# Chunked delta rule: half of the heads keep the matrices of the inverse on alternating halves of the partitions, and sums are made by identity products

## The reference, cut to what matters

```python
def step(state, inp):
    r_t, k_t, v_t, w_t, a_t, b_t = inp
    sa = jnp.einsum('bhvk,bhk->bhv', state, a_t)
    state = state * w_t[:, :, None, :] + sa[..., None] * b_t[:, :, None, :] + v_t[..., None] * k_t[:, :, None, :]
    return state, jnp.einsum('bhvk,bhk->bhv', state, r_t)
```

## Time and profile before

| | us |
|---|---|
| median of three runs | 1024.71 (1024.5 to 1026.01) |
| the profiled execution | 1027.42 |
| its span, from the first to the last instruction | 1025.6 |
| in it: PE busy | 901.2 (88%) |
| DVE busy | 448.3 (44%) |
| ACT busy | 333.9 (33%) |
| the inverse, from P2 to the start of WT | 488.27 to 525.81 |

### The profile page before, as it was taken

The page is one execution under the profiler, slowest core; times in us unless marked ns, Lnnn a source line. Parts: engine busy times, 40 slices in busy tenths (PEclk is TensorE's granted clock), DMA queues, the critical chain, the costliest instruction groups (busy, mean ns, idle before and its releaser), DMA issues.

```text
span 1025.6 us, 16699 instructions
## 1 busy us (share of the span) xinstructions
PE 901.2 (88%) x7172; PEld 614.4 (60%) x7172; DVE 448.3 (44%) x571; ACT 333.9 (33%) x440; POOL 17.4 (2%) x34
## 2 busy tenths in 40 slices
PE   9999999999999999999989997777768685777766
PEld 8889988888888889989979632221313121131311
DVE  5577778688767348895776310000001000000101
ACT  5456664565455328644433400000000000000002
POOL 1400000000000000000000000000000000000000
PEclk9999999999999999999999999888999889898989
DMA  9884424576645455442358999999999999999994
GB/s 331 228 305 158 166 84 164 164 243 206 203 165 202 167 194 176 164 167 83 114 175 333 389 420 421 421 421 422 421 422 421 423 421 422 421 422 421 421 420 184
DMA packets 87735, 294.97 MB, mean 288 GB/s; under 512 B 6383, under 2 KB 33791, under 8 KB 64624
## 3 DMA queue, kind: packets, MB, share of 16 engines
q1 hardware_dynamic: 82288, 284.18, 72.0%
q10 hardware_dynamic: 3840, 6.08, 1.6%
q0 software_dynamic: 1536, 3.68, 1.3%
HBM read 290.77 MB, written 4.10 MB: 288 GB/s over the span
## 4 chain that ended last, share of the span: by engine, by line
PE 58%; DMA 34%; DVE 5%; SPq 2%; issue 1%; ACT 1%; ACTq 0%; DVEq 0%
DMA arena<-in_w_down 16%; DMA arena<-in_w_up 15%; PE psum L1235 8%; PE psum L1104 6%; PE psum L1106 5%; PE psum L1105 5%; PE psum L1237 4%; PE psum L1262 4%; PE psum L1858 4%; PE psum L1878 3%; PE psum L1600 3%; DMA arena<-in_w_gate 3%; SPq L903 2%; PE psum L1065 1%; PE psum L1141 1%; PE psum L1140 1%
## 5 line engine op out<-in xcount | busy, mean ns | idle before, releaser
L1858 PE MATMUL psum<-arena,featL 128*32 128x512 f32 x1008 | 168.7, 652 | 61.4 <-DMA arena<-in_w_up 46.9
L2413 DVE TENSOR_TENSOR ring_rounded<-arena,hi_rounded 128x2048 fp32r<-128x2048 f32 x77 | 175.9, 2289 | 67.8 <-ACT hi_rounded L1992 66.5
L1992 ACT ACTIVATE hi_rounded<-arena 128x2048 fp32r<-128x2048 f32 x77 | 146.7, 1912 | 95.3 <-DMA arena<-in_w_in 23.0
L1858 PEld LDWEIGHTS psum<-arena,featL 128*32 128x32 f32 x1008 | 38.4, 117 | 179.2 <-DMA arena<-in_w_up 86.4
L1878 PE MATMUL psum<-arena,featT 128*32 128x512 f32 x488 | 98.4, 690 | 38.1 <-DMA arena<-in_w_down 33.3
L1235 PE MATMUL psum<-ffn_in_rounded,hi_rounded 128*128 128x512 f32 x352 | 122.5, 392 | 0.7 <-DVE ffn_in_rounded L2405 0.7
L1104 PE MATMUL psum<-hi_rounded,featT_rounded 128*128 128x256 f32 (+1 forms) x336 | 104.1, 310 | 1.2 <-DVE ring_rounded L2413 0.7
L1106 PE MATMUL psum<-hi_rounded,featL_rounded 128*128 128x256 f32 (+1 forms) x336 | 101.8, 303 | 0.0
L1105 PE MATMUL psum<-ring_rounded,featT_rounded 128*128 128x256 f32 (+1 forms) x336 | 101.8, 303 | 0.0
L1237 PE MATMUL psum<-ffn_in_rounded,ring_rounded 128*128 128x256 f32 x352 | 98.6, 280 | 0.0
L2934 DVE TENSOR_TENSOR featT<-featT,psum 128x512 f32<-128x512 f32 x8 | 8.2, 1028 | 194.1 <-PE psum L1858 194.1
(11 more groups left out here) (340 smaller groups left out, 1304.8 us busy)
## 6 DMA issues: line engine op xcount, KB each, us to landing
arena<-in_w_up SPq DMA_DIRECT2D x73, 1024.0 KB, 26.5
arena<-in_w_gate SPq DMA_DIRECT2D x70, 1024.0 KB, 26.4
arena<-in_w_down SPq DMA_DIRECT2D x58, 1024.0 KB, 26.8
arena<-in_w_in SPq DMA_DIRECT2D x14, 2048.0 KB, 8.0
arena<-in_w_down SPq DMA_DIRECT2D x5, 2048.0 KB, 7.7
arena<-in_w_out SPq DMA_DIRECT2D x3, 2048.0 KB, 8.6
arena<-in_w_in SPq DMA_DIRECT2D x4, 1024.0 KB, 9.5
arena<-in_w_down SPq DMA_DIRECT2D x8, 512.0 KB, 22.0
```

The source lines that it names most:

```text
L1858: ins = mm(psum[32 * j:32 * j + 32, MB[4 + m], :], xg[:, 4 * half + k, 32 * j:32 * j + 32], held(place(q, j), j, 512 * k), start=half == 0 ...
L1992: fn(high, view, ACT.Copy).then_inc(hi_ready, 1)
L2413: tt(low, view, high.bitcast(F32), ALU.subtract).then_inc(lo_ready, 1)
```

## The change

For the 13 steps in `MOVED` (all but TT) the odd heads now give each result to the other half of the partitions than the one their rows came from, so that from step to step their matrices change sides, while even heads stay. Each tile of such a step takes two neighbouring banks, even heads in the first and odd ones in the second, 256 columns in each. `mat("AT")` and `mat("A")` give the odd heads' A with the chunks' sides exchanged. X0 of the odd heads has to lie on the side on which A itself doesn't lie: a new filling `x0` computes A again for them there. In X1, X2 and X3 (`RENEWED`) the sum for odd heads is no longer made on DVE: PE adds X by a product with the identity into the same bank, and DVE copies it; even heads are added as before, so a tile takes two DVE instructions of 256 columns. ACT empties both banks of a tile with one instruction of 512 columns. The second chunk of `w_out_2` is split earlier, on both ACT and DVE.

```diff
+MOVED = {"P2": 1, "P2T": 1, "X1": 0, "P4": 0, "P4T": 0, "X2": 1, "P8T": 1, "X3": 0, "T16T": 1, "Z1": 1, "X4": 0,
+         "T32T": 1, "Z2": 1}
+RENEWED = ("X1", "X2", "X3")
...
@@ plan_fills
+    add("dve", "x0")
...
-            add(who, "inv", name, t)
+            if name in MOVED:
+                add(who, "inv", name, t, 0)
+                add(who, "inv", name, t, 1)
+            else:
+                add(who, "inv", name, t)
...
@@ PE
-                                cc, r = c ^ par, head_rows(par)
-                                ins = mm(banks[par][head_rows(cc), t, i, :], lhs[r, i, tokens(t, cc)], rhs[r, i, tokens(t, cc)],
+                                half, r = c ^ par, head_rows(par)
+                                cc = half ^ par if moved else half
+                                ins = mm(banks[par][head_rows(half), t, i, :], lhs[r, i, tokens(t, cc)], rhs[r, i, tokens(t, cc)],
...
-            mat("AT")
-            mat("A")
+            mat("AT", moved=True)
+            mat("A", moved=True)
+            r = head_rows(1)
+            b = begin("x0").rearrange("p (t i q) -> p t i q", t=NT, i=4)
+            for t in range(NT):
+                for i in range(4):
+                    for c in range(2):
+                        ins = mm(b[head_rows(c), t, i, :], At[r, i, tokens(t, c)], Bt[r, i, tokens(t, c)], start=True, stop=True)
+            end(ins)
...
-                    b = begin("inv", name, t).rearrange("p (i q) -> p i q", i=8)
+                    if name in MOVED:
+                        banks = [begin("inv", name, t, par)[:, 0:256].rearrange("p (i q) -> p i q", i=4) for par in range(2)]
...
-                            pe.wait_ge(x0_ready, t + 1)
+                            pe.wait_ge(x0_ready, 2)
...
+                    if name in MOVED:
+                        for i in range(4):
+                            for par in range(2):
+                                for c in range(2):
+                                    side = c ^ (par and MOVED[name])
+                                    r, o = head_rows(side), head_rows(side ^ par)
+                                    right = ident[r, r] if rhs is None else rhs[r, t, 4 * par + i, :]
+                                    ins = mm(banks[par][o, i, :], lhs[r, t, 4 * par + i, :], right, start=True,
+                                             stop=not (par and name in RENEWED), skip_group_check=True)
...
+                            if name in RENEWED:
+                                for side in range(2):
+                                    r = head_rows(side)
+                                    ins = mm(banks[1][head_rows(1 - side), i, :], ident[r, r], X[r, t, 4 + i, :], start=False,
+                                             stop=True, skip_group_check=True)
+                        end(ins)
...
@@ ACT
             high_part(first["wo2", 0], ("p2", 3, 1))
+            high_part(first["wo2", 0] + 1, ("p2", 3, 1))
...
+                        empty_pair(fn(dst[name][:, t].rearrange("p (f i) q -> p f (i q)", f=2), inverse_banks(name, t), ACT.Copy),
+                                   "inv", name, t)
-                if name == "P2T":
-                    high_part(first["wo2", 0] + 1, ("p2", 3, 1))
...
@@ DVE
             low_part(chunk_of[("wo2", 0), 0])
+            low_part(chunk_of[("wo2", 0), 1])
...
-            for t in range(NT):
-                tt(X[:, t], Ad[:, t], con("id64").unsqueeze(1).to_broadcast([P, 8, CH]), ALU.add).then_inc(x0_ready, 1)
+            tt(X[:, :, 0:4, :], Ad[:, :, 0:4, :], every("id64"), ALU.add).then_inc(x0_ready, 1)
+            wait_filled(dve, "x0")
+            empty(tt(X[:, :, 4:8, :], bank("x0").rearrange("p (t i q) -> p t i q", t=NT, i=4), every("mAd"), ALU.mult), "x0")
+            tt(X[:, :, 4:8, :], X[:, :, 4:8, :], every("id64"), ALU.add).then_inc(x0_ready, 1)
...
+                        if name in RENEWED:
+                            even, odd = (X[:, t, 4 * par:4 * par + 4, :].rearrange("p i q -> p (i q)") for par in range(2))
+                            empty(tt(even, even, bank("inv", name, t, 0)[:, 0:256], ALU.add), "inv", name, t, 0)
+                            empty(nc.vector.tensor_copy(odd, bank("inv", name, t, 1)[:, 0:256]), "inv", name, t, 1)
+                        elif name in MOVED:
+                            both = X[:, t].rearrange("p (f i) q -> p f (i q)", f=2)
+                            empty_pair(tt(both, both, inverse_banks(name, t), ALU.add), "inv", name, t)
...
-                if name == "X2":
-                    low_part(chunk_of[("wo2", 0), 1])
```

More of the change, by code:

```diff
@@ L778, in bank, with inverse_banks @@
             return psum[:, index[key] % 8, :]
+        def inverse_banks(name, t):
+            n = index["inv", name, t, 0] % 8
+            assert index["inv", name, t, 1] % 8 == n + 1
+            return psum[:, n:n + 2, 0:256]
         def bank_pair(*key):
@@ L918, in moe_stream @@
                 if first:
-                    inv = lambda *names: [("inv", *name) for name in names]
+                    inv = lambda *names: [("inv", *name, *((1,) if name[0] in MOVED else ())) for name in names]
                     wait_filled(sp, "ro", NT - 1)
@@ L1543, in _, with mat @@
             sides = {"AT": (Bt, At), "A": (At, Bt), "Aak": (f_k, At), "Arb": (Bt, f_r), "Ark": (f_k, f_r)}
-            def mat(name):
+            def mat(name, moved=False):
                 lhs, rhs = sides[name]
@@ L1583, in _ @@
                 for t in range(NT):
-                    b = begin("inv", name, t).rearrange("p (i q) -> p i q", i=8)
+                    if name in MOVED:
+                        banks = [begin("inv", name, t, par)[:, 0:256].rearrange("p (i q) -> p i q", i=4) for par in range(2)]
+                    else:
+                        b = begin("inv", name, t).rearrange("p (i q) -> p i q", i=8)
                     for need in needs:
@@ L1592, in _ @@
                         elif need == "X0":
-                            pe.wait_ge(x0_ready, t + 1)
+                            pe.wait_ge(x0_ready, 2)
+                        elif need in MOVED:
+                            wait_emptied(pe, "inv", need, t, 1)
                         else:
                             wait_emptied(pe, "inv", need, t)
+                    if name in MOVED:
[7 more added lines that the diff above has]
+                                             stop=not (par and name in RENEWED), skip_group_check=True)
+                                    if (par, i) == (0, 3) and c == 1:
+                                        end(ins)
[4 more added lines that the diff above has]
+                                             stop=True, skip_group_check=True)
+                        end(ins)
+                        continue
                     for i in range(8):
@@ L1958, in _ @@
             empty = lambda ins, *key: a.empty("act", ins, *key)
+            empty_pair = lambda ins, *key: a.empty_pair("act", ins, *key)
             def squares(n, ready, warmed=False):
@@ L2249, in _ @@
                     for t in range(NT):
-                        wait_filled(act, "inv", name, t)
-                        empty(fn(dst[name][:, t].rearrange("p i q -> p (i q)"), bank("inv", name, t), ACT.Copy), "inv", name, t)
-                if name == "P2T":
-                    high_part(first["wo2", 0] + 1, ("p2", 3, 1))
+                        wait_filled(act, "inv", name, t, 1)
+                        empty_pair(fn(dst[name][:, t].rearrange("p (f i) q -> p f (i q)", f=2), inverse_banks(name, t), ACT.Copy),
+                                   "inv", name, t)
                 if name == "Z1":
@@ L2759, in _ @@
                 masked(Ad, "A", "mAd", par)
-            for t in range(NT):
-                tt(X[:, t], Ad[:, t], con("id64").unsqueeze(1).to_broadcast([P, 8, CH]), ALU.add).then_inc(x0_ready, 1)
+            every = lambda m: con(m).unsqueeze(1).unsqueeze(1).to_broadcast([P, NT, 4, CH])
+            tt(X[:, :, 0:4, :], Ad[:, :, 0:4, :], every("id64"), ALU.add).then_inc(x0_ready, 1)
+            wait_filled(dve, "x0")
+            empty(tt(X[:, :, 4:8, :], bank("x0").rearrange("p (t i q) -> p t i q", t=NT, i=4), every("mAd"), ALU.mult), "x0")
+            tt(X[:, :, 4:8, :], X[:, :, 4:8, :], every("id64"), ALU.add).then_inc(x0_ready, 1)
             token_rows("V")
```

13 lines of the change are left out of this document (9 added, 4 removed).

## The result

| | median us | range, runs | ratio to before, 95% |
|---|---|---|---|
| before | 1024.61 | 1023.97 to 1026.51, 6 | |
| after | 1030.09 | 1028.82 to 1031.39, 6 | 1.0048, 1.0038 to 1.0058 |

A forecast was written before the change was run, and what follows sets the result against it. PE's instruction supply was taken to bound the inverse, about 4.03 us per 256-instruction block; +4.0 us for products and +0.4 us for waits, +4.6 us by block edges, gave 1029.3 us from 1024.71, range 1023.5 to 1032.5.

The forecast's parts named there:

- The end moves with the stretch: Inverse: a microsecond won or lost there reaches the end as a microsecond, as the last 476 us run at full DMA rate.
- rival B: No change: transfers take in the longer stretch, or gains outside the block limit meet the 4 us; 1024.7 us, 14%.
- Blocks at 4.03 us: PE in the inverse: each 256-instruction block costs at least about 4.03 us; eight whole ones from 492.15 reach 524.4.
- the delay at the start: P2T's start behind DVE's early split: 2.2 us late, nearly all disappearing because the next block comes no earlier than 496.2.
- The tail: From the second Q tile to WT: nothing short of instructions, 6.0 us as before.
- Instructions: PE in the inverse: 256 for added products, +4.0 us, and some 25 waits, +0.4 us; plain count 1.1 blocks.
- WT at 530.4: Start of the WT products, the forecast's mark: 530.4 us instead of 525.81, +4.6 us.
- what the forecast said would show it: Trace after: many "issue" pieces of 1 to 2 us, one per block, nine or so packets, busy share below 93%, WT at 530.
- DVE and ACT: Inverse: early split fits idle time; P2T starts at 491.8 and 493.25; X1 to X3 cost DVE 0.9 us more, beside PE's waits.
- A: Faster: supply doesn't stop PE, both stops go, DVE's queue sets the pace; WT at 522.4, -3.4 us, 1021.3 us, 13%.
- DVE's late start: Start of the inverse: the early low_part, 2.29 us on DVE, pushes masks and copies back, delaying P2T by 2.2 us.
- C: Much slower: doubled demand makes each fetch late, eight blocks at 4.4 us, +7.5 us, 1032 us, 11%.

The follow-up runs named there:

- e0: The changed kernel run once more, unaltered; 1029.98 us, ratio to before 1.0028 to 1.0062.
- e2: The changed kernel with 218 wait instructions, for semaphores long met, among the products of the moved tiles; 1037.99 us, ratio 1.0101 to 1.0136.
- e4: The changed kernel without the 48 identity products of X1, X2 and X3, 192 instructions fewer; 1029.35 us, ratio 1.0027 to 1.0061.
- e8: The changed kernel with 64 long-met waits on PE in the earlier feed-forward stage, shifting later block borders; 1032.23 us, ratio 1.0061 to 1.0102.
- e5: The changed kernel with the split of the second w_out_2 chunk back in its old places; 1030.72 us, ratio 1.0033 to 1.0067.
- e3: The changed kernel with 176 long-met waits on PE in the earlier feed-forward stage, shifting later block borders; 1032.90 us, ratio 1.0054 to 1.0086.
- e9: The changed kernel with 128 long-met waits on PE in the earlier feed-forward stage, shifting later block borders; 1031.62 us, ratio 1.0052 to 1.0086.
- u2: The kernel before with X1 and P4 made by joint products of 128 columns, 128 instructions fewer; 1025.49 us, ratio 0.9997 to 1.0014.
- e6: The kernel before with 64 extra short products of 8 columns in the inverse, 256 instructions more; 1028.63 us, ratio 1.0018 to 1.0051.

## Why the prediction was right, point by point

**The end moves with the stretch.** The forecast took a microsecond in the stretch for one at the end. The stretch grew by 4.8 us (4.0 in e0), the time by 5.5. From WT to the end it is 499.7 us before and 498.5 after, in single profiles. The transfers took nothing in, and rival B is out. The close match of 4.8 and 5.5 us is partly chance, since the profiled execution of the kernel before (1027.42 us) is a slow one of its kernel: between the two profiled executions WT moved by 4.0 us and the end by 2.8 (1025.6 to 1028.4). In each of the fourteen profiles it is 498.1 to 500.2 us, also where WT moved by 13 us (e2), so within one execution the rule holds to some 2 us. The medians in the table follow it less well: in e4 and e8 the time grew 3 us more than the stretch of the one execution that was profiled.

**Blocks at 4.03 us.** Eight blocks lay between the first border and the one in the Q products, as forecast; they took 32.82 us (491.12 to 523.94), forecast 32.2. But the equality hides two errors. The seven undisturbed ones took 3.97 us. The first took 5.00: PE stood in it until 492.20 us waiting for vraw, its next packet came 2.46 us after the border instead of 1.2 to 1.8, and so the delay at the start doesn't "nearly all disappear", about 1 us of it stays. The sum was saved by the stretch having begun 0.8 us earlier than before.

**The tail.** From the last border to WT 5.91 us, forecast 6.0.

**Instructions.** 256 for products were counted rightly; the waits added are 12, not 25: 268 instructions, 1.05 blocks for 1.1. From AT to WT there were 11 packets, ten before. The mark "WT at 530.4" was 529.85; the pieces named "issue" were 0.5 to 1.7 us, eight of them, one per block; PE's busy share fell from 93% to 68% (27.93 of 40.83 us from 489.02 to WT). But for the sizes of the waits and of WT, this is what the forecast said would show it.

**DVE and ACT.** P2T started at 490.75 and 492.20 behind the V copies and vraw, each about 1 us before the forecast times (491.8, 493.25), since everything ahead lay earlier. In the order of time of DVE (start, us, instruction, idle before):

```profile
484.36 2.87 DVE L2770 TENSOR_TENSOR arena<-psum,cst 128x512 f32<-128x512 f32 x4
487.26 0.69 DVE L2809 TENSOR_TENSOR arena<-arena,cst 128x512 f32<-128x512 f32 x1
...
490.64 1.42 DVE L2817 TENSOR_TENSOR rt<-psum,st 128x512 f32<-128x512 f32 x2
493.78 0.42 DVE L2826 TENSOR_TENSOR arena<-arena,psum 128x256 f32<-128x256 f32 x1 [1.73 <-PE psum L1630]
```

The early split fills the gap that stood in front of the masks, the short additions take the 0.42 us read from the earlier trace rows, and DVE waits for PE behind them. No step of ACT shows in the chain as anything but its copies.

**The rivals.** A fell with the eight stops. The early start of P2T that would separate the supply from DVE's late start was not reached in e5, so that the delay leaves 1 us is read from one block and not from an experiment. The rule of the Trainium skill (Runtime: NRT & Kernel Launch, "Instruction fetch mechanics"), that crossing a block's border is mostly hidden, doesn't hold where a block is worked off in less than 4 us. The Trainium skill's bound of up to two times (TensorEngine Tiling (Array Packing), "Theoretical Speedup") agrees with the busy time, 3.85 us of a block on two quadrants and 2.2 on four, and gains nothing here. C's 4.4 us a block weren't reached by the kernel as it stands (3.97), but the runs with other borders come to 1031.6 to 1032.9 us, C's time. In e3 a late packet, two stops of 2 us and a lower clock in the stretch stand beside it, which the forecast didn't have; which of them costs the 3 us isn't separated, and in e8 and e9 the stretch doesn't show the loss at all. That the forecast of 1029.3 fits 1030.1 so well therefore owes something to where the borders of this program happen to lie.

## What to carry to other kernels

Where many small instructions follow each other on PE, count them as well as the work: here a block of 256 took about 4 us however little of it was work, so packing the array paid nothing and the added products cost. Where the array is busy for most of the 4 us anyway, fewer instructions bring nothing either (u2). Pieces named "issue" at equal distances in instructions, with one packet on the instruction queue between two, are the sign. And compare two versions of such a stretch at more than one place of its borders (a few waits far ahead that cost nothing will shift them) before a difference of 0.3% is believed.

## What was not expected of the hardware

- A single border costs the wait for a request, a packet and a restart: 1.47 + 1.14 + 1.36 = 3.97 us in the seven blocks, much the same beside 4 GB/s (3.73 and 3.90 us) and beside 194 GB/s (4.12 us) on the DMA queues.
- The packet can come later in a block in which PE waits for another engine: 2.46 us after the border in the block that waited for vraw, 3.0 us in e8's block from 498.51 us, 4.2 us in e3's from 513.76 us, where the clock was 0.62. It needn't: in the block of the kernel after that starts at 504.33 us, with a wait for ACT, it came after 1.2 us. What holds it back stays open.
- 64, 128 or 176 wait instructions among products of 512 columns cost nothing there, 218 in the inverse cost 8.7 us.
- Stops of 1.8 to 2.2 us were followed by a granted clock of 0.5 to 0.8 in e3, e5, e8 and e9; in e2 it fell to 0.50 behind stops of 1.3 us and less. The kernel after, with stops up to 1.70 us, kept 1.00, and so did e4 with one of 1.81 us. So the length of a stop alone doesn't tell.
- On two quadrants a 64x64 record takes 29 ns with 64 columns and, in the tile of e6, with 8, and 54 ns with 128 (64 of them in 3.4 us).
